# Layer norms by blocks of 128 tokens, ple_proj ahead of v, na_out ahead of retention's turn, in a fp32 three-block forward pass

## What is computed

```python
def layer_norm(x, g, b):
    mu = mean(x); var = mean(square(x - mu))
    return (x - mu) * rsqrt(var + 1e-5) * g + b

def first_block(x, p, ...):
    x = layer_norm(alpha * x + mlstm_mixer(x), ln_g[0, 0], ln_b[0, 0])
    x = layer_norm(alpha * x + peer_ffn(x), ln_g[0, 1], ln_b[0, 1])
    x = x + sigmoid(x @ ple_w_gate[0]) * (p[0] @ ple_w_proj[0])
    x = layer_norm(alpha * x + mla_mixer(x), ln_g[1, 0], ln_b[1, 0])
    x = layer_norm(alpha * x + peer_ffn(x), ln_g[1, 1], ln_b[1, 1])
    x = x + sigmoid(x @ ple_w_gate[1]) * (p[1] @ ple_w_proj[1])
    return x

def token_mixing(u):
    y_ret = (silu(rg) * rms(retention(q, k, v))) @ w_ret_out
    y_na = neighborhood_attention(nq, nk, nv) @ w_na_out
    return (sigmoid(g_ret) * y_ret + sigmoid(g_na) * y_na) @ w_out
```

## Time and profile before

| | us |
|---|---|
| median of 3 runs | 2710.41 |
| lowest, highest run | 2710.34, 2713.19 |
| the profiled execution, its own time | 2716.81 |
| its span in the profile | 2715.0 |
| PE busy | 2628.0 (97%) |
| DVE busy | 1693.2 (62%) |
| ACT busy | 1477.2 (54%) |
| POOL busy | 625.6 (23%) |

### The profile page before, as it was taken

One profiled execution on the slowest core, in us unless ns is written; L12 is line 12 of the kernel. 1 busy time (PEld: TensorE's weight loads), 2 busy tenths in 40 slices (PEclk: granted clock), 3 DMA queues, 4 the chain that ended last, 5 costly groups with the idle time before them and its releaser, 6 DMA issues.

```text
span 2715.0 us, 42429 instructions
## 1 busy us (share of the span) xinstructions
PE 2628.0 (97%) x14442; PEld 2236.8 (82%) x14442; DVE 1693.2 (62%) x3127; ACT 1477.2 (54%) x2534; POOL 625.6 (23%) x336
## 2 busy tenths in 40 slices
PE   8999999999999998999999999999999999989998
PEld 6679999998888875779999988888878877766886
DVE  3457847886555564359657876555557746554774
ACT  4334568875544444444578875444445545553553
POOL 0006877760000000007877740000000000000000
PEclk9899999999999998999999999999999999999999
DMA  6145544446556553235544446555556555434454
GB/s 215 63 147 173 184 163 143 145 142 200 192 193 192 193 184 107 97 132 182 182 156 143 145 149 203 193 193 193 193 174 193 190 174 176 138 98 155 156 191 149
DMA packets 124028, 447.44 MB, mean 165 GB/s; under 512 B 14280, under 2 KB 14920, under 8 KB 123648
## 3 DMA queue, kind: packets, MB, share of 16 engines
q1 hardware_dynamic: 119808, 434.16, 48.6%
q0 software_dynamic: 2608, 9.08, 1.1%
q10 hardware_dynamic: 1488, 2.59, 0.3%
HBM read 444.74 MB, written 1.05 MB: 164 GB/s over the span
## 4 chain that ended last, share of the span: by engine, by line
PE 91%; DVE 4%; ACT 3%; issue 1%; DMA 1%; ACTq 0%; DVEq 0%
PE ps L773 41%; PE ps L729 19%; PE ps L734 10%; PE ps L922 4%; PE ps L745 4%; PE ps L751 4%; PE ps L748 4%; DVE X L1641 1%; PE ps L680 1%; PE ps L807 1%; PE ps L976 1%; DVE big L1641 1%; PE ps L893 1%; ACT w_hi L401 1%; DVE stats L1734 0%
## 5 line engine op out<-in xcount | busy, mean ns | idle before, releaser
L401 ACT CAST w_hi<-ring 128x1024 fp32r<-128x1024 f32 (+1 forms) x808 | 847.5, 1049 | 842.6 <-PE ps L773 529.3
L413 DVE TENSOR_TENSOR w_lo<-ring,w_hi 128x1024 fp32r<-128x1024 f32 (+1 forms) x629 | 768.2, 1222 | 578.9 <-ACT w_hi L401 570.2
L413 POOL TENSOR_TENSOR w_lo<-ring,w_hi 128x1024 fp32r<-128x1024 f32 (+1 forms) x179 | 429.2, 2398 | 1679.9 <-ACT w_hi L401 1679.9
L773 PE MATMUL ps<-w_hi,x_parts 128*128 128x512 f32 x2976 | 750.0, 393 | 9.9 <-DVE x_parts L2010 4.7
L773 PEld LDWEIGHTS ps<-w_hi,x_parts 128*128 128x128 f32 x2976 | 558.1, 190 | 132.2 <-issue 11.0
L729 PE MATMUL ps<-x_parts,w_hi 128*128 128x512 f32 x2208 | 564.4, 397 | 0.1
L729 PEld LDWEIGHTS ps<-x_parts,w_hi 128*128 128x128 f32 x2208 | 395.9, 189 | 71.4 <-ACT w_hi L401 0.3
L773 PE MATMUL ps<-w_lo,x_parts 128*128 128x512 f32 x1488 | 403.4, 390 | 0.3 <-DVE w_lo L413 0.3
L773 PEld LDWEIGHTS ps<-w_lo,x_parts 128*128 128x128 f32 x1488 | 279.9, 189 | 59.8 <-DVE w_lo L413 1.3
L734 PEld LDWEIGHTS ps<-x_parts,w_lo 128*128 128x128 f32 x2208 | 300.9, 190 | 22.9
L734 PE MATMUL ps<-x_parts,w_lo 128*128 128x256 f32 x2208 | 307.4, 282 | 0.0
(11 more groups left out here) (244 smaller groups left out, 2293.5 us busy)
## 6 DMA issues: line engine op xcount, KB each, us to landing
ring<-in_u SPq DMA_DIRECT2D x256, 512.0 KB, 3.2
ring<-in_v SPq DMA_DIRECT2D x256, 512.0 KB, 4.3
ring<-in_ffn_in SPq DMA_DIRECT2D x88, 512.0 KB, 3.3
ring<-in_ffn_out SPq DMA_DIRECT2D x44, 512.0 KB, 3.9
ring<-in_wq SPq DMA_DIRECT2D x32, 512.0 KB, 3.3
ring<-in_ple_gate SPq DMA_DIRECT2D x16, 512.0 KB, 4.5
SC<-in_rows POOLq DMA_DIRECT2D x11, 512.0 KB, 4.5
ring<-in_a_qk SPq DMA_DIRECT2D x8, 512.0 KB, 4.7
```

Of the source, the lines that this page charges most:

```text
L401: nc.scalar.copy(part(w_hi, i)[:, used(name)], tile(i)[:, used(name)]).then_inc(tiles_hi, 1)
L413: eng.tensor_tensor(part(w_lo, i)[:, at], tile(i)[:, at], part(w_hi, i)[:, at], ALU.subtract).then_inc(tiles_low[LOW[n][0]], 1)
L773: mm = nc.tensor.matmul(acc[:, 2 * tb + f, 0:cnt], x[:, k + c, tb * P:(tb + 1) * P], part(w, i)[:, at:at + cnt], start=(first and n == 0 a ...
```

## The change

It does five things.

1. Layer norms run block by block. DVE leaves the first block's sum in X, the second's in the accumulator. ACT subtracts the first block's mean (new `roots_by_block`), POOL multiplies it by the gain (new `scale_first`), DVE centres the second block by halves. DVE makes a diagonal of each block's inverse root (`root_of`), and PE's turn multiplies X by that diagonal instead of the identity, onto slots in which it has put the bias by a product of the bias row and the identity (new `turn_normed`, in the place of `turn_over`). X itself is scaled later, between the next stage's tiles (`scaled_rows`). Fillers are 8 for all four.
2. ple_proj stands ahead of v, in the stream and on PE, and goes to four slots instead of the accumulator; ACT copies them out during v's last tiles. v opens and closes the accumulator with its own first and last tile, whose two blocks are announced one after the other; the eight zero matmuls are gone.
3. `ml_first` orders its six products by the rows of the array they use: 845, 847 (8 rows), 853, 854 (64), 846, 849 (128, the mask, now last). The decay's slot is announced after the scores'.
4. na_out stands ahead of ret_out in the stream, and on PE ahead of retention's turn; ACT takes g_na's sigmoid before the root, and the early loading of the root's table is gone; DVE gates na_out before it takes retention's low parts.
5. POOL's queue is unchanged but for `scale_first`.

```diff
-FILLERS = {"ml_out": 24, "ln0_0": 28, "x1": 12, "ln1_0": 28, "rms1": 40, "rms2": 40, "merged": 8, "rms3": 40}
+FILLERS = {"ml_out": 24, "ln0_0": 8, "ln0_1": 8, "x1": 12, "ln1_0": 8, "ln1_1": 8, "rms1": 40, "rms2": 40, "merged": 8, "rms3": 40}
...
-PEER_TILES = [("wq", 16), ("keys", 2), ("u", EXPERT_TILES), ("v", EXPERT_TILES), ("ple_proj", 2), ("ple_gate", 8)]
+PEER_TILES = [("wq", 16), ("keys", 2), ("u", EXPERT_TILES), ("ple_proj", 2), ("v", EXPERT_TILES), ("ple_gate", 8)]
...
-    + [("ret_out", 8), ("na_out", 4), ("mix_out", 8)]
+    + [("na_out", 4), ("ret_out", 8), ("mix_out", 8)]
...
+            def scale_first(name):
+
+                n = LN_TURNS.index(name)
+                pool.wait_ge(rows_in, 16 * sum(ROW_SETS[:n + 1]))
+                for f in range(2):
+                    at = slice(512 * f, 512 * f + 512)
+                    pool.wait_ge(first_centred, 2 * n + f + 1)
+                    nc.gpsimd.tensor_tensor(X[:, 0, at], X[:, 0, at], rows[:, 0, at], ALU.mult
+                                            ).then_inc(first_scaled, 1)
...
                 take_low(pool, f"wq{layer}", 0)
+                scale_first(f"ln{layer}_0")
                 experts(layer)
                 load_rows(2 * layer + 1, (tiles_gated, tiles_with_gates(layer, EXPERT_TILES - 1)))
                 load_p(layer)
                 take_low(pool, f"ple_gate{layer}", 0)
+                scale_first(f"ln{layer}_1")
...
+            def turn_normed(name):
+
+                n, first = LN_TURNS.index(name), SLOT[f"turn_{name}"]
+                pe.wait_ge(rows_in, 16 * sum(ROW_SETS[:n + 1]))
+                for q in range(4):
+                    slot_free(pe, first + q)
+                    for c in range(2):
+                        nc.tensor.matmul(bank(first + q)[:, c * T:(c + 1) * T].rearrange("p (a b) -> p a b", a=TB),
+                                         rows[:, 1, (2 * q + c) * P:(2 * q + c + 1) * P],
+                                         ident[:, None, :].to_broadcast([P, TB, P]), start=(c == 0), stop=False)
+                for _ in range(FILLERS[name]):
+                    nc.tensor.matmul(bank(first), zeros[:, 0:P], zeros[:], start=False, stop=False)
+                for f in range(2):
+                    for tb in range(TB):
+                        if f == 0:
+                            pe.wait_ge(diag_ready, TB * DIAG[name] + tb + 1)
+                        if tb == 0:
+                            pe.wait_ge(first_scaled, 2 * n + f + 1)
+                        else:
+                            pe.wait_ge(turn_ready, 2 * TURN[name] + f + 1)
+                        for q in range(2 * f, 2 * f + 2):
+                            for c in range(2):
+                                at = (2 * q + c) * P
+                                mm = nc.tensor.matmul(bank(first + q)[:, (2 * c + tb) * P:(2 * c + tb + 1) * P],
+                                                      X[:, tb, at:at + P], diag[:, tb], start=False,
+                                                      stop=(tb == TB - 1 and c == 1))
+                            if tb == TB - 1:
+                                full(mm, first + q)
...
-                for b in range(4):
-                    nc.tensor.matmul(acc[:, b, :], zeros[:, 0:P], zeros[:], start=True, stop=False)
-                with pe.Fori(0, EXPERT_TILES // BODY, 1) as turns:
-                    for j in range(BODY):
-                        pe.wait_ge(staged, turns * BODY + (EXPERT_TILES * layer + j + 1))
-                        split_wide(f"v{layer}", j, (x_hi, x_lo), j, False, False, turns)
-                for b in range(4):
-                    mm = nc.tensor.matmul(acc[:, b, :], zeros[:, 0:P], zeros[:], start=False, stop=True)
-                    if b % 2:
-                        mm.then_inc(acc_full, 1)
-
                 pe.wait_ge(p_in, 16 * (layer + 1))
-                to_acc(f"ple_proj{layer}", tokens(pT), 2)
-                turn_over(f"ln{layer}_1", X)
+                for c in range(2):
+                    tile_here(pe, TILE[f"ple_proj{layer}"] + c)
+                for n in range(4):
+                    s = SLOT[f"ple_proj{layer}"] + n
+                    slot_free(pe, s)
+                    tb, at = n // 2, 512 * (n % 2)
+                    for c in range(2):
+                        mm = nc.tensor.matmul(bank(s), pT[:, c, tb * P:(tb + 1) * P],
+                                              tile(TILE[f"ple_proj{layer}"] + c)[:, at:at + 512],
+                                              start=(c == 0), stop=(c == 1))
+                        if c == 0 and n in (0, 3):
+                            begins_tile(mm)
+                    full(mm, s)
...
+                turn_normed(f"ln{layer}_1")
...
+            moved(pe, SLOT[("na", "out", H8 - 1)])
+            to_acc("na_out", tokens(na_oT), 4)
             turn_over("ret", ret_y.rearrange("p t h n -> p t (h n)"))
             split_to_acc("ret_out", turn="ret")
-            moved(pe, SLOT[("na", "out", H8 - 1)])
-            to_acc("na_out", tokens(na_oT), 4)
...
+            def roots_by_block(name):
+
+                n = LN_TURNS.index(name)
+                act.wait_ge(mean_ready, n + 1)
+                for f in range(2):
+                    at = slice(512 * f, 512 * f + 512)
+                    S.activation(X[:, 0, at], X[:, 0, at], ACT.Identity, bias=col[:, 2, 0:1]).then_inc(first_centred, 1)
+                    square_roots(1, f)
...
-                    sqrt_table()
-                    highs("g_na", 2 * h + 1, 2 * h + 2, following="ret_out")
+                    take_high(act, "g_na", 2 * h + 1)
...
+            from_acc("g_na", lambda tb: sig_na[:, tb, :], ACT.Sigmoid)
             square_roots(8)
-            from_acc("g_na", lambda tb: sig_na[:, tb, :], ACT.Sigmoid)
+            take_high(act, "ret_out", 0)
...
+            def root_of(tb):
+
+                counts["sqrt"] += 1
+                dve.wait_ge(sqrt_done, counts["sqrt"])
+                step(V.reciprocal(col[:, 1, tb:tb + 1], col[:, 1, tb:tb + 1]))
+                wait()
+                V.tensor_scalar(diag[:, tb], ident[:], col[:, 1, tb:tb + 1], None, ALU.mult).then_inc(diag_ready, 1)
+
+            def layer_norm(name, turn):
+
+                for tb, total in enumerate((X[:, 0, :], acc_rows(1))):
                     acc_here(dve, name, tb)
-                    V.scalar_tensor_tensor(out=X[:, tb, :], in0=X[:, tb, :], scalar=DN_ALPHA, in1=acc_rows(tb),
-                                           op0=ALU.mult, op1=ALU.add).then_inc(acc_moved, 1)
-                    acc_moved_up_to(name, tb)
+                    ins = V.scalar_tensor_tensor(out=total, in0=X[:, tb, :], scalar=DN_ALPHA, in1=acc_rows(tb),
+                                                 op0=ALU.mult, op1=ALU.add)
+                    if tb == 0:
+                        ins.then_inc(acc_moved, 1)
+                        acc_moved_up_to(name, 0)
+                    else:
+                        step(ins)
+                        root_of(0)
+                        wait()
                     for f in range(2):
-                        step(V.bn_stats(stats[:, 2 * tb + f, :], X[:, tb, 512 * f:512 * f + 512]))
+                        step(V.bn_stats(stats[:, 2 * tb + f, :], total[:, 512 * f:512 * f + 512]))
+                    wait()
+                    step(V.bn_aggr(mv[:, tb, :], stats[:, 2 * tb:2 * tb + 2, :]))
+                    wait()
+                    if tb == 0:
+                        V.tensor_scalar(col[:, 2, 0:1], mv[:, 0, 0:1], -1.0, None, ALU.mult).then_inc(mean_ready, 1)
+                    ts(col[:, 0, tb:tb + 1], mv[:, tb, 1:2], NORM_EPS, None, ALU.add)
+                    wait()
+                    dve.sem_inc(sqrt_wanted, 1)
+                rows_here()
+                for f in range(2):
+                    at = slice(512 * f, 512 * f + 512)
+                    V.scalar_tensor_tensor(out=X[:, 1, at], in0=total[:, at], scalar=mv[:, 1, 0:1],
+                                           in1=rows[:, 0, at], op0=ALU.subtract, op1=ALU.mult).then_inc(turn_ready, 1)
+                    if f == 0:
+                        root_of(1)
+                dve.wait_ge(turn_ready, 2 * TURN[turn] + 2)
+                dve.sem_inc(acc_moved, 1)
...
+            def scaled_rows(turn, tb):
+
+                slot_here(dve, SLOT[f"turn_{turn}"] + 3)
+                stt(X[:, tb, :], X[:, tb, :], col[:, 1, tb:tb + 1], rows[:, 1, :], ALU.mult, ALU.add)
                 wait()
-                for tb in range(TB):
-                    step(V.bn_aggr(mv[:, tb, :], stats[:, 2 * tb:2 * tb + 2, :]))
-                wait()
-                ts(col[:, 0, 0:TB], mv[:, 0:TB, 1], NORM_EPS, None, ALU.add)
-                wait()
-                dve.sem_inc(sqrt_wanted, 1)
-                rows_here()
-                for tb in range(TB):
-                    stt(X[:, tb, :], X[:, tb, :], mv[:, tb, 0:1], rows[:, 0, :], ALU.subtract, ALU.mult)
```

(54 more changed lines are left out.)

64 lines of the change are left out of this document (38 added, 26 removed).

## The result

| | before | after |
|---|---|---|
| median, us | 2712.2 (6 runs, 2710.3 to 2717.6) | 2724.0 (6 runs, 2718.0 to 2727.2) |
| ratio, 95% interval | | 1.004 (1.003 to 1.0049) |
| profiled execution, its span, us | 2716.8, 2715.0 | 2724.05, 2722.0 |

The change makes the kernel 11.8 us slower. That is only 0.4%, but the interval excludes 1. The forecast was +16.4 us. The profiled execution of before lay 4.6 us over its median, that of after on it, so the two spans differ by 7.0 only.

What follows compares the result with a forecast made beforehand. The prediction took the kernel to be bound by PE, with 91% of the chain of waits. Its terms, -11.9 + 33.6 - 4.3 - 1.0 = +16.4, took 2710.4 to 2727 us, range 2716 to 2742.

Steps and rivals of the forecast that it cites:

- Part 2: Between u and v: ple_proj moved ahead of v makes PE wait for p; v starts 16.8 us later, twice, +33.6 us.
- p's landing: Between u and v: p, issued behind the row loads, takes 5.3 us to load and lands at 653.5.
- Products and clock: ple_proj before v: its fp32 matmuls take 7.0 us, plus 2.9 us lost to the lower clock after PE's idling.
- Part 1: The four layer norms: gains of 3.4 us in ln0_0, 2.7 in ln1_0, 2.9 each in ln0_1 and ln1_1; -11.9 us.
- the sum for one norm: Layer norm ln0_0: from DVE's first pass, 14.0 us before and 10.6 after, the second group starting at 7.8; gain 3.4.
- Part 3: mLSTM heads: three fewer row-count changes among six products, 0.18 us each in 8 heads; -4.3 us, bounds 0 to -6.
- Part 4: na_out ahead of retention's turn: PE waits about 4.0 us as before; net -1.0 us, bounds +2 and -4.5.
- g_na's casts: At g_na's last cast: the table load ahead of it goes, and with it PE's 1.49 us wait.
- The middle: na_out to ret_out: 14.0 + 2.9 us, transposes 2.2, two gate passes 2.4, first low part 1.0, ret_out 21.8.
- the list of what is won: na_out ahead of retention's turn: wins the table load before g_na's last cast (1.49 us wait) and one 1.2 us gate pass.
- the one in which p costs little: Rival at ple_proj: p lands near its lower bound, clock returns at once, +11.9 twice; 2717 us, chance 0.12.
- Faster: p is in time: Rival between u and v: POOL gets to p under u, v only 3.7 us late per layer; 2701 us, chance 0.04.

Runs made afterwards that it cites:

- the kernel of the early p: The changed kernel with p's load issued ahead of the two row loads in POOL's queue; 2698.5 us, ratio to before 0.9946.
- the early table: The changed kernel with p's load ahead of the row loads, plus the root's table loaded before the wait for the mean in three later norms; 2700.4 us, 0.9948.

## Why the prediction was right, and where it was off

The forecast was 2727 with 2716 to 2742, the time 2724. The mechanism was the one named: the queue of POOL, with p behind the row loads behind the last gated tile.

- **Part 2, +33.6; measured +29.3.** p's landing was forecast 10.35 us after u's end, it was 10.2 and 10.0. Products and clock: 9.9 forecast, 9.04 and 9.06 measured. The rest of the difference is that 1.1 us a layer at v's end, which the prediction had booked under part 1 (as 1.8), come with this part. The Trainium skill, page DMA: Bandwidth & Descriptors, section Anatomy of one DMA — SWDGE (gpsimd) path, would have had p land after an estimated 2.6 us; the trace has 643.52 less 638.13, 5.4 us, behind two row loads, and with nothing ahead of it in the kernel of the early p 4.7 and 4.0. The measurement decides.
- **Part 1, -11.9; measured 5 to 9.** The step that was over-sized is the sum for one norm. Of the 11.9, 2.2 belong to part 2. The second group of products starts 8.2 us after DVE's first pass in ln0_0 and not 7.8, since DVE's first diagonal (taken at 0.5 with its reciprocal, measured 0.9) ends only behind POOL's product. In the other three it starts after 8.75 and not 8.45, since DVE waits 0.85 us for the root and not 0.65. Moving the table load away doesn't give back the whole wait, because the diagonal then takes 0.70 there too: 1.6 us came back in three norms (forecast 2.0). The last product so ends 0.6 us late in ln0_0 and 0.4 in each of the others, 1.7 in sum. By the stretches 7.1 of 9.7 were gained; where the other 0.9 went is open. The Trainium skill's drain of 1380 ns (page ScalarE: Activation LUTs, section What ACT_TABLE_LOAD costs) appears in no row here: in the rows above the load at 2505.48 takes 1.28 and its ACTIVATE starts at 2506.78.
- **Part 3, -4.3; measured -5.2.** 0.18 us per change of the row count was 0.20 in the traced pitch (0.60 for three), 4.8 in 8 heads.
- **Part 4, -1.0; measured -3.5.** g_na's casts gave 1.3, near the forecast 1.49. The middle came out at -0.6 (-0.8 in the trace of the whole change) where the terms summed to about +0.5. The step that failed is the list of what is won: the prediction followed ACT's table loads up to retention and stopped, and the load that fell away lies one stage further, worth 1.2 us of PE's wait at the post norm.
- The errors had one sign in parts 2 to 4 (-4.3, -0.9, -2.5) and the other in part 1 (+3.1, by the -8.8 that closes the sum): 16.4 became 11.8. That 2727 came within 3 us of 2724 is in part luck: the kernel before came out 1.8 us above the 2710.4 from which the forecast started, and a part 1 forecast too well made up for some of what the others were forecast too badly. Of those errors 2.2 us are one amount, booked under part 1 instead of part 2. The rivals: the one in which p costs little is wrong by its reason (the load took its usual time), though its 2717 was not far. "Faster: p is in time" gave 2701 for a kernel in which POOL gets to p early. With the two lines swapped that is 2698.5.

## What to carry to other kernels

When a step moves forward in one engine's program, look up for each operand when it arrives, not only whether it was ever waited for: an operand that was always in time may have been so by the slack of the old place, and the cure may be one swap in another engine's queue. Follow the ACT table past the edit to the next function that needs it, since a changed order of two functions moves loads in stages that the diff doesn't touch. And a short step is best cut to the size of the gap that it covers.

## What was not expected of the hardware

Equal instructions behind equal pauses take unequal times, by when the clock comes back. After about 6 us without work for PE the same twelve fp32 products took 8.19 us in the changed kernel,

```profile
1065.72 2.82 PE L1026 MATMUL ps<-ident,big 128*128 128x128 f32 x12 [6.32 <-DVEq L2209]
1069.55 8.19 PE L703 MATMUL ps<-ring,big 128*128 128x512 f32 x12 [1.01 <-ACT big L1538]
```

at a clock of 0.50 and then 0.72,

```profile
1069.00:1073.00 4.00, 3.45 (x4) 1.51 (x5) 0.00 (x0) 0.31 (x2) 0.00 (x0) 0.50 0.00 0
1073.00:1077.00 4.00, 4.00 (x8) 1.77 (x7) 0.00 (x0) 0.00 (x0) 0.00 (x0) 0.72 0.23 52
```

and 5.39 in the kernel of the early p, where the clock was back at 1.00 from 1057 on. From kv_q_down's end to b_out's first product it was 60.5 us before, 57.7 after, 55.5 with the early p and 60.1 with the early table, though no edit lies there.

Such a gain can be paid for next door. In the kernel of the early p the clock had fallen in the shorter pauses ahead of kv_q_down, where the changed kernel kept 1.00:

```profile
1028.00:1032.00 4.00, 3.93 (x12) 3.35 (x13) 2.66 (x5) 1.53 (x3) 0.00 (x0) 0.50 0.12 18
```

kv_q_down took 19.4 us there and 17.2 in the changed kernel, so both need the same from its first product to b_out's: 74.8 and 75.0 us. Before it was 77.8, and 77.4 with the early table. These 2.8 us between before and after, with 1.4 in the stages around them, are the 4.2 us in the fifth row of the stage table. They are nearly what the two spans lack against the two medians, and more than the early table had to win; that they are the reason for either isn't shown.
